# Two feed-forward parts of the second transformer layer as seven block products, with weight sums made by accumulating DMAs

## What is computed

```python
def swiglu(h, w_gate, w_up, w_down):      # h 512x1024, w_gate and w_up 1024x2816, w_down 2816x1024
    return (silu(h @ w_gate) * (h @ w_up)) @ w_down

h2 = modulate(rms_norm(x, norm2_g[l]), sh2, sc2)
x = x + gt2 * swiglu(h2, w_ffn_gate[l], w_ffn_up[l], w_ffn_down[l])
```

## Time and profile before

| | us |
|---|---|
| median of 3 runs (lowest, highest) | 2407.35 (2402.33, 2410.02) |
| the profiled execution | 2405.56 |
| its span | 2403.7 |
| layer 1's hidden tiles and `add_to_x`, all three parts | about 1576 to 1941 |

### The profile page before, as it was taken

The page is one execution under the profiler, slowest core; times in us unless marked ns, Lnnn a source line. Parts: engine busy times, 40 slices in busy tenths (PEclk is TensorE's granted clock), DMA queues, the critical chain, the costliest instruction groups (busy, mean ns, idle before and its releaser), DMA issues.

```text
span 2403.7 us, 32947 instructions
## 1 busy us (share of the span) xinstructions
PE 2326.5 (97%) x12159; PEld 1988.4 (83%) x12159; DVE 1645.6 (68%) x2525; ACT 1190.4 (50%) x1910; POOL 224.6 (9%) x338
## 2 busy tenths in 40 slices
PE   7999999999999999999999999999999999999999
PEld 3888887888888998998778777898888877877787
DVE  5786776789688877878686777754333456389864
ACT  5647777733333431432647776343222355477641
POOL 0100000010001112221100000100000010011120
PEclk9999999999999999999999999999999999999999
DMA  7421111174334237347221112523222333521253
GB/s 289 149 77 47 47 47 47 55 276 146 114 124 146 99 117 244 128 145 252 97 88 53 49 53 69 181 80 105 97 97 97 105 107 134 182 87 67 84 202 118
DMA packets 71381, 282.41 MB, mean 117 GB/s; under 512 B 9040, under 2 KB 9104, under 8 KB 69824
## 3 DMA queue, kind: packets, MB, share of 16 engines
q1 hardware_dynamic: 42336, 162.94, 19.3%
q0 software_dynamic: 28896, 117.46, 13.8%
HBM read 245.76 MB, written 33.55 MB: 116 GB/s over the span
## 4 chain that ended last, share of the span: by engine, by line
PE 78%; DVE 9%; ACT 7%; issue 4%; DMA 2%; POOL 0%; SPq 0%; ACTq 0%; DVEq 0%
PE ps L217 21%; PE ps L218 21%; PE ps L219 21%; DVE w_lo L213 2%; PE ps L1282 1%; PE ps L1216 1%; PE ps L1283 1%; PE ps L1284 1%; PE ps L1223 1%; DMA ada_raw<-in_ada 1%; DVE inv L1446 1%; ACT w_hi L206 1%; PE ps L1265 1%; ACT pr L1345 1%; PE ps L894 1%
## 5 line engine op out<-in xcount | busy, mean ns | idle before, releaser
L217 PE MATMUL ps<-h_hi,w_hi 128*128 128x512 f32 (+2 forms) x1592 | 577.6, 363 | 15.9 <-DVE h_lo L1585 6.8
L218 PE MATMUL ps<-h_lo,w_hi 128*128 128x512 f32 (+2 forms) x1592 | 567.1, 356 | 0.0
L219 PE MATMUL ps<-h_hi,w_lo 128*128 128x512 f32 (+2 forms) x1592 | 566.1, 356 | 0.0
L213 DVE TENSOR_TENSOR w_lo<-w_raw,w_hi 128x1024 fp32r<-128x1024 f32 x256 | 319.1, 1248 | 188.3 <-ACT w_hi L206 187.8
L206 ACT ACTIVATE w_hi<-w_raw 128x1024 fp32r<-128x1024 f32 x256 | 269.2, 1053 | 236.1 <-PE ps L219 215.6
L217 PEld LDWEIGHTS ps<-h_hi,w_hi 128*128 128x128 f32 x1592 | 302.8, 190 | 67.2 <-issue 15.6
L219 PEld LDWEIGHTS ps<-h_hi,w_lo 128*128 128x128 f32 x1592 | 302.1, 190 | 44.3
L218 PEld LDWEIGHTS ps<-h_lo,w_hi 128*128 128x128 f32 x1592 | 303.1, 190 | 42.5 <-issue 2.4
L217 PE MATMUL ps<-q_hi,w_hi 128*128 128x512 f32 x720 | 255.6, 355 | 1.6 <-DVE q_lo L1606 1.6
L218 PE MATMUL ps<-q_lo,w_hi 128*128 128x512 f32 x720 | 256.3, 356 | 0.0
L219 PE MATMUL ps<-q_hi,w_lo 128*128 128x512 f32 x720 | 254.5, 354 | 0.0
(11 more groups left out here) (449 smaller groups left out, 4282.6 us busy)
## 6 DMA issues: line engine op xcount, KB each, us to landing
w_raw<-in_stream SPq DMA_DIRECT2D x288, 512.0 KB, 3.2
wt_x<-in_ada_t POOLq DMA_DIRECT2D x24, 512.0 KB, 3.8
wt_h<-in_ada_t POOLq DMA_DIRECT2D x20, 512.0 KB, 5.3
ada_raw<-in_ada SPq DMA_DIRECT2D x4, 2048.0 KB, 17.9
wt<-in_ada_t POOLq DMA_DIRECT2D x16, 512.0 KB, 3.7
x_keep<-x POOLq DMA_DIRECT2D x8, 768.0 KB, 7.7
gates<-th_g POOLq DMA_DIRECT2D x16, 384.0 KB, 2.6
gates<-sg POOLq DMA_DIRECT2D x24, 256.0 KB, 2.3
```

What stands on the lines that cost most here:

```text
L213: nc.vector.tensor_tensor(w_lo[:, u % 3, :], raw[:, u % 2, :], w_hi[:, u % 3, :].bitcast(F32), ALU.subtract).then_inc(lo_ready, 1)
L217: nc.tensor.matmul(out_ap, lh, rh, start=start, stop=False)
L218: nc.tensor.matmul(out_ap, lh, rl, start=False, stop=False)
L219: return nc.tensor.matmul(out_ap, ll, rh, start=False, stop=stop)
```

## The change

`FF_PARTS` of layer 1 becomes (6, 8, 8). Its part 0 is still made by `hidden_late`, its parts 1 and 2 by `hidden_pairs`, with blocks of 256 tokens. Layer 0 keeps its code.

`TokenBlocks` makes layer 1's token blocks. At steps 8 to 11 of part 0's `hidden_late` VectorE adds `n_hi` and `n_lo` up again to full precision (`rejoined`) and makes t1 to t4 from that; during the first steps of `add_to_x` ScalarE and VectorE split them. The four plain blocks are views of `n_hi` and `n_lo`.

`PairsAgain` replaces the weight sums of GpSimd and VectorE. For each pair GpSimd issues four plain DMAs of half a unit, 128x512 floats or 256 KB, from `stream` (`load`) and four accumulating DMAs of the same size (`add_up`): c onto the tiles `ac` and `cd` (from `stream`), then `ac` onto `acd`, then `acd` onto `abcd` (both from on-chip memory), each waiting for the one before. Three sets of the four tiles are in turn. `load` of pair p waits until VectorE has made all low parts of pair p-3. The low parts of blocks 0, 1 (together) and 5 now free the slots of `w_raw`.

```diff
-FF_PARTS = ((6, 8, 8), (8, 8, 6))
+FF_PARTS = ((6, 8, 8), (6, 8, 8))
...
+        class TokenBlocks:
+            ORDER = ("t1", "t3", "t2", "t4")
+            lows, half = 4, SEQ // 2
+            second_sign = ALU.subtract
...
+            def sums(self, dve, n, scaled):
+                f, late, whole = self.full, self.late, r_h["rejoined"]
+                combine = nc.vector.tensor_tensor
+                if n == 8:
+                    dve.wait_ge(scaled.sem, scaled.base + 8)
+                    dve.wait_ge(late.whole_lo.sem, late.whole_lo.base + CH)
+                if n in (8, 9):
+                    for c in (4 * n - 32, 4 * n - 30):
+                        if c < CH - 2:
+                            two = slice(c, c + 2)
+                            combine(whole[:, two, :], late.n_hi[:, two, :].bitcast(F32), r_kv["n_lo"][:, two, :].bitcast(F32),
+                                    ALU.add).then_inc(self.joined.sem, 1)
...
+                if n == 10:
+                    dve.wait_ge(self.joined.sem, self.joined.base + 5)
+                    combine(f["t1"], f["b11"], f["b12"], ALU.subtract).then_inc(self.summed.sem, 1)
+                    combine(f["t3"], f["b22"], f["b12"], ALU.subtract).then_inc(self.summed.sem, 1)
+                if n == 11:
+                    dve.wait_ge(self.summed.sem, self.summed.base + 2)
+                    combine(f["t2"], f["t3"], f["b11"], ALU.add).then_inc(self.summed.sem, 1)
+                    dve.wait_ge(self.summed.sem, self.summed.base + 3)
+                    combine(f["t4"], f["t2"], f["b21"], ALU.subtract).then_inc(self.summed.sem, 1)
+
+            def high_of(self, act, j):
+                if j < 4:
+                    name = self.ORDER[j]
+                    act.wait_ge(self.summed.sem, self.summed.base + j + 1)
+                    nc.scalar.activation(self.hi[name], self.full[name], ACT.Copy).then_inc(self.high.sem, 1)
...
+        class PairsAgain(Pairs):
...
+            def mark(self, k):
+                return lo_ready if k in (1, 5) else self.low.sem
...
+            def set_of(self, p):
+                if p % 3 == 2:
+                    return [r_h["w_sums_h"][:, n, :] for n in range(2)] + [r_s["w_sums_s"][:, n, :] for n in range(2)]
+                return [r_h["sums_%d" % (p % 3)][:, n, :] for n in range(4)]
...
+            def load(self, pool, p):
+                u, (ac, cd, acd, abcd) = self.base + 2 * p, self.set_of(p)
+                a, b, d = stream[u][:, 0:512], stream[u][:, 512:1024], stream[u + 1][:, 512:1024]
+                if p >= 3:
+                    pool.wait_ge(self.low.sem, self.low.base + 4 * (p - 2))
+                for tile, block in ((ac, a), (cd, d), (acd, d), (abcd, b)):
+                    pool.dma_start(tile, block).then_inc(self.loaded[p % 2].sem, 16)
+
+            def add_up(self, pool, p):
+                u, (ac, cd, acd, abcd) = self.base + 2 * p, self.set_of(p)
+                c = stream[u + 1][:, 0:512]
+                here = self.loaded[p % 2]
+                pool.wait_ge(here.sem, here.base + 64 * (p // 2 + 1))
+                pool.dma_start(ac, c, accum_op=ALU.add).then_inc(self.with_c[0].sem, 16)
+                pool.dma_start(cd, c, accum_op=ALU.add).then_inc(self.with_c[1].sem, 16)
+                for s in self.with_c:
+                    pool.wait_ge(s.sem, s.base + 16 * (p + 1))
+                pool.dma_start(acd, ac, accum_op=ALU.add).then_inc(self.of_three.sem, 16)
+                pool.wait_ge(self.of_three.sem, self.of_three.base + 16 * (p + 1))
+                pool.dma_start(abcd, acd, accum_op=ALU.add).then_inc(self.of_four.sem, 16)
+                pool.wait_ge(self.of_four.sem, self.of_four.base + 16 * (p + 1))
+
+            def wait_sum(self, act, p, k):
+                s = {2: self.of_three, 3: self.with_c[0], 4: self.with_c[1], 6: self.of_four}[k]
+                act.wait_ge(s.sem, s.base + 16 * (p + 1))
...
             def pool(e):
                 made = 7 + sum(DOWN_PASSES) if part == 2 else 0
+                if not side:
+                    e.wait_ge(blocks.summed.sem, blocks.summed.base + 4)
+                    e.wait_ge(pairs.low.sem, pairs.low.base)
+                    pairs.load(e, 0)
+                    pairs.load(e, 1)
+                    for p in range(N):
+                        pairs.add_up(e, p)
+                        if p + 2 < N:
+                            pairs.load(e, p + 2)
+                    return
...
-            blocks, pairs, spill = (Blocks(norm), None, Spill()) if layer == 0 else (None, None, None)
+            blocks, pairs, spill = (Blocks(norm), None, Spill()) if layer == 0 else (TokenBlocks(norm, u0), None, None)
...
-                pairs = Pairs(u0 + CH, FF_PARTS[0][part + 1]) if layer == 0 and part < 2 else None
+                pairs = (PairsAgain if layer else Pairs)(u0 + CH, FF_PARTS[layer][part + 1]) if part < 2 else None
```

More of the change, by code:

```diff
@@ L1974, in wait_here, with hidden_pairs @@
                     dve.wait_ge(self.x_here.sem, self.x_here.base + 16 * (9 + j))
-        def hidden_pairs(pairs, blocks, before, side, spill, part):
+        def hidden_pairs(pairs, blocks, before, side=None, spill=None, part=0):
             nonlocal u0
@@ L2031, in act @@
                             silu_of(p, right, 2)
-                        if k == 6 and p == 0 and part == 1:
+                        if side and k == 6 and p == 0 and part == 1:
                             side.condition(e)
@@ L2070, in middle_sums @@
                     if at < 7:
[L2071 removed]
+                        ins = nc.vector.tensor_tensor(halves(qf[:, p, 0:w]), ps[:, at:at + 2, 0:half], twice_over(ff[:, p % 2, left]), ALU.add)
                     else:
@@ L2081, in ups @@
                     if at < 7:
-                        ins = nc.vector.tensor_tensor(halves(ff[:, p % 2, :]), ps[:, at:at + 2, 0:HALF], twice_over(qf[:, p, left]), ALU.add)
+                        ins = nc.vector.tensor_tensor(halves(ff[:, p % 2, 0:w]), ps[:, at:at + 2, 0:half], twice_over(qf[:, p, left]), ALU.add)
                     else:
@@ L2130, in dve @@
                             gate_right(p)
-                        if k == 0 and (p or part == 2):
+                        if side and k == 0 and (p or part == 2):
                             side.one_pass(e)
@@ L2135, in dve @@
                 hidden_low(N - 1)
-                if part == 1:
+                if side and part == 1:
                     side.wt_out = su[:, :, :].rearrange("p a n -> p (a n)")[:, 0:D]
@@ L2250, in act @@
                         late.whole_high(e, c)
-                    if blocks and 4 <= n < 12:
+                    if blocks and not late.whole and 4 <= n < 12:
                         blocks.shift(e, n - 4)
@@ L2289, in dve @@
                         late.times(e, c)
-                    if blocks and 3 <= n < 11:
+                    if blocks and not late.whole and 3 <= n < 11:
                         blocks.times(e, n - 3)
+                    if blocks and late.whole:
+                        blocks.sums(e, n, scaled)
                     if side:
@@ L2308, in hidden_late @@
             engines = dict(pe=pe, act=act, dve=dve)
-            if side and opening:
+            if opening and side:
                 engines["pool"] = pool
```

138 lines of the change are left out of this document (113 added, 25 removed).

## The result

The changed kernel takes 2494.8 us (median of 4 runs, 2489.2 to 2498.2), the kernel before 2405.3 beside it (4 runs, 2402.3 to 2410.0): a ratio of 1.0369, with an interval of 1.0355 to 1.0383. It is slower by 3.7%; forecast were 2418.5 us and a range of 2394 to 2440. The sign was right, the size was not, and the range missed it by 55 us.

The account below looks back on a forecast made before the run. TensorE's matmuls were taken as the bound. Gain 12.8 us against 24.0 of lateness from GpSimd's chain made 11.2 more: 2405.56 to 2416.8 on the profiled execution, 2418.5 on the median; range 2394 to 2440.

Parts of the forecast that it names:

- the products: Layer 1's feed-forward: sixteen tiles of 174.1 us become 16 pairs of 84 matmuls, 161.3 us; gain 12.8 us.
- The token sums: VectorE, steps 8 to 11 and add_to_x: four times 2.5 us plus four of 1.2, all hidden, cost 0.
- lead: Sets 0 and 1 added up long before a part's first pair; pair 3's load then starts 3.4 us into the part.
- T: Period of GpSimd's turn per pair: 14.7 us forecast, 12.0 to 17.7, against 10.08 allowed; break-even 13.6.
- L: Last step of GpSimd's turn, about 3 us, subtracted because pair 6's a+c+d is ready before it.
- S: Time at which a part's first pair starts; pair 6's a+c+d is wanted 61.9 us after it.
- plain turn: GpSimd's turn without the adding: six queued transfers 8.0, noticing 0.3, two lone transfers of 2.8; 13.9 us.
- adding: Accumulating in GpSimd's four DMAs per pair: 0.8 us taken, a quarter of the 3.3 at most.
- pair 7: Last pair of a part: no load issued before it, needs under 10 us, so adds no lateness.
- Rival 2: GpSimd's adding costs a full second transfer: T = 17.7, 39.4 us slower, 2447; chance 0.15 for it or worse.
- Rival 1: GpSimd's chain hidden, T up to 12.0: 2394.6 us; T under 12.8 was given a chance of 0.27.
- Rival 3: Narrow matmuls miss 0.120 us or VectorE hands over late: 2407; chance 0.25 together with T of 12.8 to 14.3.

Follow-up runs that it names:

- the run with two waits: Changed kernel with a+b+c+d issued together with the next pair's additions of c, and the four loads moved behind a+c+d; 2448.9 us.
- The plain copies: Changed kernel with its four accumulating DMAs per pair made plain copies, same order and waits, no sums formed; 2435.52 us.

## Why the prediction was wrong in size

**Right.** What bounds the kernel, and the products: 12.8 us of gain were forecast, and the kernel without the additions is 15.1 faster (2403.7 - 2388.6, one execution each). 84 x 0.120 = 10.08 is met. **VectorE**: 8.8 us per pair or less when back to back; it is busy 48.43 of 60.00 us in the kernel without additions (1692 to 1752), 8.1 per pair. **The token sums** are hidden: between 1625 and 1662 TensorE waits 1.5 us, once, before and after alike. The place and the kind of the loss too: GpSimd's turn of waits, a high part that waits for a DMA, TensorE behind it.

**Wrong: the formula's inputs.** The lateness of pair 6's third block was reckoned as lead + 5T - L - 61.9. In part 2, where the lead came out nearly as forecast (the load of pair 3 at S + 3.9, with S = 1862.33), these rows of GpSimd give a T of 19.6, the mean of five turns; the rows are the load of pair 3, a+b+c+d of pair 6, and what follows its landing:

```profile
1866.18 2.18 POOL L2107 DMA_DIRECT2D sums<-in_stream  x4 [3.66 <-DVE w_lo L2064]
...
1960.57 0.85 POOL L2121 DMA_DIRECT2D sums<-sums  x1 [2.70 <-DMA sums<-sums]
1964.10 0.85 POOL L2115 DMA_DIRECT2D sums<-in_stream  x1 [2.68 <-DMA sums<-sums]
```

With L = 3.5 the formula says 3.9 + 98.0 - 3.5 - 61.9 = 36.5 us. Measured are 1961.81 - (1862.33 + 60.48 + 2.88) = 36.1. So the model holds; these terms of it didn't:

| | forecast, us | measured, us | worth in both parts, us |
|---|---|---|---|
| plain turn | 13.9 | 15.7, 15.2 | |
| adding, per turn | 0.8 (at most 3.3) | 4.2, 4.4 | |
| T in all (less 0.5 per part for L) | 14.7 (12.0 to 17.7) | 19.9, 19.6 | 49 |
| load of pair 3 | S + 3.4 | S + 17.9, S + 3.9 | 15 |
| lateness added by pair 7 | 0 | 5.1 and 5.3 | 10 |

The measured pairs are those of part 1 and part 2. With the 24.0 forecast the terms make 98, against 98.8 measured (2487.4 - 2388.6).

- **The adding** was mis-sized most. Of the 5 us by which T was short, it makes 3.5 and the plain turn 1.5. There was no row, so a quarter of its high end was taken, and that high end was "a second transfer of 0.83 for each of the four", 3.3 us. The engines' time grew by about as much for each (0.72 to 1.61), but GpSimd's wait, not engine time, is the term of the sum: it grew by 1.0 us for a lone addition and by over 2 for the two of c behind the loads, 4.3 in all. The bound was put on the wrong quantity, and so the range too, which ended at T = 17, fell short of 19.6.
- **The lead.** The step "sets 0 and 1 are added up long before, in the `add_to_x` ahead (32 us or more)" failed in part 1. GpSimd starts at 1653.86, when the last token sum is made, 27.6 us ahead of S = 1681.5, and the eight loads and two turns took 45.6. Even by the forecast's own terms they would have needed 7.4 for the eight loads, 11.4 for a turn without loads of its own (14.7 - 4 x 0.83) and 14.7 for the next, 33.5 of the 31.0 (27.6 + 3.4) that there were; the prediction never set the two side by side. Part 1 ends 15 us later than part 2 for it (pair 6's block is 51.3 late, not 36.1).
- **Pair 7.** "Needs under 10" left out that a+b+c+d of pair 6 stands ahead of it: from that issue at 1794.92 to the notice of a+c+d of pair 7 at 1810.10 are 15.2 us.

Two of its sums are off by 0.1 in rounding (T = 12.9 is 13.0, and 17.7 is 17.8 by its own terms), which changes nothing.

**The clock** was not in the prediction. In the stretch 1690 to 1800 the granted clock is 0.78, and behind the wait of 7.81 us above TensorE runs its next 18 matmuls at the lower of its two levels, 1.2 GHz (the changed kernel's timeline of TensorE; from 1720.82 on at 2.4 GHz again):

```profile
1716.99 0.42 PE L220 MATMUL ps<-token_blocks,w_hi 128*128 128x256 f32 x1
1717.20 0.41 PE L221 MATMUL ps<-token_blocks,w_lo 128*128 128x256 f32 x1
...
1720.62 0.37 PE L219 MATMUL ps<-token_blocks,w_hi 128*128 128x256 f32 x1
1720.82 0.28 PE L220 MATMUL ps<-token_blocks,w_hi 128*128 128x256 f32 x1
1720.94 0.28 PE L221 MATMUL ps<-token_blocks,w_lo 128*128 128x256 f32 x1
```

They start 0.213 us apart, not 0.120: about 1.9 us for this wait; behind the others it was 13 to 28 matmuls, and behind the one of 3.49 us none. Over the page, TensorE is busy 22.5 us more than without the additions (2332.4 - 2309.9), and 76.2 idle + 22.5 = 98.7 is the whole loss. That sum is an account, not a second cause: between two waits of the chain the pairs take exactly a turn of GpSimd's, 10.08 + 1.9 + 7.8 = 19.8, so at full clock TensorE would only have waited longer. Only behind the last wait of a part does it cost time of its own: in part 1 that is the wait of 3.49 us, with no fall, in part 2 one of 3.01 with 13 slow matmuls, some 1.2 us. This is argued from the rows; no run took the clock's fall away.

**The rivals.** Rival 2 (adding costs a full second transfer, 2447) had the right mechanism and still too little. Rival 1 (hidden) needed T up to 12.0; no turn with all eight transfers came under 13.8, and their engines' time alone is about 12.7. Rival 3 (matmuls not at 0.120, or VectorE late) is refuted by the kernel without additions.

**Left open.** Why two additions from `stream` take 7.3 us with no load ahead of them, where a lone one on chip takes 3.5: SyncE's stream runs beside them, and no run took it away. How much of the 5 us of the run with two waits belongs to the wait and how much to the place of the loads is not shown either.

## What to carry to other kernels

For a queue that waits for its own transfers, two sums have to fit the period of its consumer: the issue-to-notice times that stand in a row, and the time that all transfers of a turn take from the DMA engines. Here they were 19.6 and 12.7 us against 10.08. The plain copies show the first alone (15.2 to 15.7 against 8.9); with the last two additions on VectorE (0.69 us each) both fit. Reckon the start of such a chain with the same turn: two turns and the first loads have to fit between the event that releases it and its first consumer. Where an operation has no row in the trace, bound the quantity that the sum uses (the wait), not a related one (the engine time), and leave the range open on that side.

## What the runs showed of the hardware

- In the turns shown an accumulating DMA of 256 KB between tiles on chip is noticed 3.5 us after its issue, a plain one 2.5; its issue takes GpSimd 0.85 us, not 0.54. Over all 64 transfers, half of them from `stream`, an addition takes 1.61 us of the 16 DMA engines' time, a copy 0.72, and it makes 144 packets in place of 80 (43232 and 39136 in the queue's rows, 34016 without either).
- The DMA engines can be 0.97 busy for 50 us at 262 GB/s with additions among the transfers, and TensorE waits for nobody.
- After a wait of 7.8 us TensorE ran 18 matmuls of 256 columns at half clock, after others of 2.5 to 8.1 us 13 to 28, after one of 3.49 us none: the length of the wait alone doesn't tell.
- VectorE's 512-wide steps with both inputs in on-chip memory outside PSUM take up to 2.8 times as long beside GpSimd's additions (0.68 and 1.89 us), those with one input in PSUM keep their time.
